# Delta rule of a hybrid decoder: matrix products of three chunks grouped into fewer bursts

## The chip, the cores and the metric

The kernel runs as one program on one core of one Trainium2 chip. The time is the device time of one launch in microseconds, from the first to the last instruction of the program and what lies around them; lower is better. Engines are named as the profile names them: PE is TensorE, DVE is VectorE, ACT is ScalarE, POOL is GpSimd, SP is SyncE.

## What is computed

One step of a one-layer decoder trunk: a projection of 1024 columns in, a mixer with two branches (RWKV-7 time mixing and retention), an output projection, and a mixture of 16 experts. It runs on 528 prompt tokens (16 of them learned) and 8 sample tokens, all in float32. The change lies in the RWKV-7 branch, whose recurrence over tokens is, for each of 8 heads of width 64:

```python
def step(S, inp):
    r_t, w_t, k_t, v_t, kk_t, a_t = inp
    sa = jnp.einsum('bhvk,bhk->bhv', S, -kk_t)
    S = (S * w_t[:, :, None, :]
         + sa[..., None] * (kk_t * a_t)[:, :, None, :]
         + v_t[..., None] * k_t[:, :, None, :])
    y = jnp.einsum('bhvk,bhk->bhv', S, r_t)
    return S, y
```

The state S is returned too. The kernel computes this in chunks of tokens: inside a chunk the tokens' mutual influence is a triangular system, which is solved by an inverse, and only the state goes from chunk to chunk.

## The kernel before

All engines walk through one list of steps, `STEPS`, made by `order()`; each engine does its own part of each step in the order of the list and waits on semaphores for the others. So the order of the list is the order on every engine.

The prompt's 528 tokens make nine chunks: eight of 64 and one of 16 (`CHUNKS`). The 8 heads lie in four pairs, two heads on the 128 partitions. The steps of a chunk c are:

- `wk_e` (ACT): decay factors by exponentials; `wk_p` 0 to 3 (DVE): scaled keys `bk` and the pair of scaled kk and r, `ar`. The last one raises `s_ab`.
- `wk_a` (PE, L1614 to L1632): products of three kinds. The 64x64 matrices between tokens (called A below, L1614), their 32x32 diagonal tiles both ways up (D, L1618 and L1622), and transposes of values and keys (K, L1629 and L1632). DVE then masks D into `tp` (two operations) and A into `ak` (two operations of 128x512); ACT copies K.
- `wk_x` and `wk_t` with b = 2, 4, 8, 16 (X2, T2, X4, ... below): the inversion of the 32x32 tiles by doubling. X (L1643) is 32 products of 32x32 and DVE masks the result; T (L1653 and L1656) is 64 products, at b = 16 only 32, and DVE adds them. Each of these needs the DVE answer to the one before.
- the state chain: `wk_r` (R, L1671 with 128x64 operands and L1676 with 64x64), answered by ACT; `wk_sa` (SA, L1686, upper tiles), ACT; `wk_y` (Y, L1695), DVE; `wk_sb` (SB, L1703, lower tiles), ACT; `wk_s` (S, L1713, L1719 and L1724), answered by DVE with the new state and by ACT with y.

The counts above are the records of the trace: each product of float32 leaves two. The shapes in the trace's rows are those of the weights (rows*columns of the array used) and of the moving data.

The loop runs c from -1 to 7. In an iteration the inversion of chunk c + 1 goes beside the state chain of chunk c. Behind each group of small products ("burst") `take(n, b)` appends n units of other work, "filling": a unit is two products of 128x128 by 128x260 (four records, about 0.88 us), parts of the jobs `j_proj` (L1389), `j_f` (L1425) and `j_bb` (L1402), held in the list `fill`, 146 units in all. `TAKES` says how many units follow each of the nine bursts. When `fill` is empty, `take` gives tiles of branch A, `j_ba` (eight records of L1794). `take` also puts in small steps of `side`: the sample tokens' steps, and the norm behind the recurrence (`j_mean` L1754, `j_var` L1765 and L1761, `ln_r` reciprocals, `j_bc` L1774 and L1779, `ln_b`, `ln_g`). Where c is 5 the loop takes units until a whole job is done; those counted in `owed` are taken off later.

After the loop come the last chunk's R, SA and S, with two takes of two between them, then the rest of `side` by `LAST` with one `j_ba` tile behind each group, then for each of eight tiles the second half of branch A (`j_ba` with 1), which needs all seven parts of the norm (`s_ya`), then the output projection `j_out`, the routing and the experts.

Every DVE operation of the loop is recorded at L2143 or L2146, ACT's at L1893, L2035 and L2056, since helpers make them.

## Time and profile before

| | us |
|---|---|
| median of three runs | 786.96 |
| lowest and highest | 785.82, 788.06 |
| the profiled execution | 785.98 |
| its span, first to last instruction | 784.2 |

| stage, us from the start of the span | what runs |
|---|---|
| 0 to 261 | norm, projections, retention |
| 261 to 515 | the chunk loop |
| 515 to 545 | rest of the norm, branch A |
| 545 to 628 | output projection, routing |
| 628 to 784 | experts, output |

A row of the timeline gives the start, the length (of several instructions: from the first start to the last end), the engine, the line, the operation, out<-in, shapes, the count, and in brackets how long the engine had been idle and who ended that. Lengths of matmuls overlap, so prices are read from the distance of starts.

### The profile page before, as it was taken

The numbers are of one execution on the slowest core, as the hardware profiler recorded it, in microseconds if no ns is written. First come the engines' busy times: TensorE is split into PE (matmuls) and PEld (weight loads), VectorE is DVE, ScalarE is ACT, GpSimd is POOL, SyncE is SP. The second block draws the span as 40 slices with busy tenths as digits, with TensorE's granted clock in tenths as the row PEclk, the third lists the DMA queues.
The fourth block names the chain that finished last, engine by engine and source line by source line (L and its number), as shares of the span: only waits on it lengthen the run. The fifth ranks groups of instructions, "written<-read, shape, count | busy, mean of one in ns | idle before, by whom it ended". The sixth has DMA issues, their size and how long they took to land.

```text
span 784.2 us, 19872 instructions
## 1 busy us (share of the span) xinstructions
PE 751.3 (96%) x8472; PEld 529.5 (68%) x8472; DVE 426.5 (54%) x853; ACT 209.7 (27%) x491; POOL 49.5 (6%) x70
## 2 busy tenths in 40 slices
PE   6999999999999999999999999999999599999995
PEld 5887777787778777777787777778888433333331
DVE  5966667788778574656556565355213432212145
ACT  4222222254525212222222332210031501111144
POOL 0000000000000000010000000000000111221221
PEclk9999999999999999999999999999999789999998
DMA  9562432432211101212422102084934689999965
GB/s 324 191 203 94 148 124 100 178 111 83 79 54 55 55 29 58 69 45 90 129 86 58 55 31 83 13 309 138 413 123 186 237 333 400 393 402 389 370 210 206
DMA packets 38134, 130.43 MB, mean 166 GB/s; under 512 B 6267, under 2 KB 16763, under 8 KB 33184
## 3 DMA queue, kind: packets, MB, share of 16 engines
q1 hardware_dynamic: 32544, 115.07, 39.1%
q0 software_dynamic: 5504, 14.10, 6.1%
q8 instruction: 68, 1.11, 0.6%
q14 instruction: 18, 0.15, 0.1%
HBM read 111.13 MB, written 18.66 MB: 166 GB/s over the span
## 4 chain that ended last, share of the span: by engine, by line
PE 88%; DVE 4%; DMA 4%; issue 2%; ACT 1%; POOL 0%; SPq 0%; POOLq 0%; DVEq 0%; ACTq 0%
PE psum L1444 23%; PE psum L1425 12%; PE psum L1794 10%; PE psum L2740 9%; PE psum L2774 4%; PE psum L1402 4%; DVE arena L2143 3%; PE psum L1377 2%; PE psum L1389 2%; PE psum L1643 2%; PE psum L1656 1%; PE psum L2720 1%; PE psum L1653 1%; PE psum L1614 1%; PE psum L1567 1%
## 5 line engine op out<-in xcount | busy, mean ns | idle before, releaser
L2143 DVE TENSOR_TENSOR arena<-arena 128x268 f32<-128x268 f32 (+13 forms) x322 | 176.5, 548 | 46.3 <-ACT arena L1893 27.6
L1444 PE MATMUL psum<-arena 128*128 128x268 f32 x784 | 188.3, 392 | 0.0
L1444 PEld LDWEIGHTS psum<-arena 128*128 128x128 f32 x784 | 145.3, 189 | 33.3 <-issue 6.7
L1893 ACT ACTIVATE arena<-psum 128x268 f32<-128x268 f32 (+7 forms) x207 | 83.0, 410 | 260.0 <-PE psum L1444 138.6
L1425 PE MATMUL psum<-arena 128*128 128x260 f32 x392 | 101.3, 396 | 0.0
L2143 DVE TENSOR_TENSOR arena<-psum,arena 128x256 f32<-128x256 f32 (+7 forms) x151 | 60.5, 405 | 67.2 <-PE psum L1656 22.5
L1794 PE MATMUL psum<-arena 128*128 128x260 f32 x384 | 88.4, 384 | 1.6 <-DVE arena L2143 1.3
L2740 PE MATMUL psum<-arena 128*32 128x512 f32 (+1 forms) x640 | 87.2, 608 | 0.5 <-DVE arena L2905 0.3
L1794 PEld LDWEIGHTS psum<-arena 128*128 128x128 f32 x384 | 71.1, 189 | 15.3 <-issue 3.2
L2905 DVE TENSOR_TENSOR arena<-psum,arena 128x256 f32<-128x256 f32 (+2 forms) x38 | 24.3, 663 | 103.2 <-ACT arena L2809 90.7
L1425 PEld LDWEIGHTS psum<-arena 128*128 128x128 f32 x392 | 69.6, 189 | 14.4 <-issue 2.8
L1893 ACT ACTIVATE arena<-arena 128x260 f32<-128x260 f32 (+11 forms) x121 | 49.1, 451 | 98.8 <-PE psum L1806 56.2
L2740 PEld LDWEIGHTS psum<-arena 128*32 128x32 f32 (+1 forms) x640 | 25.5, 117 | 58.6 <-issue 58.0
L2146 DVE SCALAR_TENSOR_TENSOR arena<-arena 128x536 f32<-128x536 f32 (+8 forms) x77 | 48.9, 635 | 8.0 <-ACT arena L1893 3.2
L2774 PE MATMUL psum<-arena 128*32 128x512 f32 (+1 forms) x288 | 40.2, 596 | 0.0
L2146 DVE SCALAR_TENSOR_TENSOR arena<-psum,arena 128x260 f32<-128x260 f32 (+2 forms) x23 | 10.1, 441 | 46.9 <-PE psum L1794 40.2
L1402 PE MATMUL psum<-arena 128*128 128x260 f32 x128 | 33.3, 396 | 0.0
L2143 DVE TENSOR_TENSOR arena<-arena,psum 128x260 f32<-128x260 f32 (+4 forms) x35 | 17.6, 514 | 19.7 <-PE psum L1425 16.0
L2146 DVE SCALAR_TENSOR_TENSOR arena<-arena,psum 128x260 f32<-128x260 f32 x32 | 13.7, 427 | 24.2 <-PE psum L1402 12.3
L2809 ACT ACTIVATE arena<-psum 128x256 f32<-128x256 f32 x12 | 4.6, 385 | 79.8 <-PE psum L2740 67.6
L1111 POOL DMA_INDIRECT arena<-u_rows,ids x12 | 12.3, 1022 | 207.7 <-issue 149.8
L2774 PEld LDWEIGHTS psum<-arena 128*32 128x32 f32 (+1 forms) x288 | 10.8, 115 | 21.3 <-issue 21.3
(234 smaller groups left out, 690.9 us busy)
## 6 DMA issues: line engine op xcount, KB each, us to landing
arena<-in_w_gu SPq DMA_DIRECT2D x16, 2048.0 KB, 20.4
arena<-in_w_in SPq DMA_DIRECT2D x45, 512.0 KB, 3.9
arena<-in_w_dn SPq DMA_DIRECT2D x16, 1024.0 KB, 18.2
arena<-in_w_out SPq DMA_DIRECT2D x2, 2048.0 KB, 14.7
arena<-in_x SPq DMA_DIRECT2D x8, 268.0 KB, 5.8
arena<-arena SPq DMA_DIRECT2D x16, 134.0 KB, 4.4
arena<-in_x SPq DMA_DIRECT2D x1, 2144.0 KB, 14.5
arena<-arena SPq DMA_DIRECT2D x4, 520.0 KB, 6.5
```

The costliest lines, as they stand in the source:

```text
L1377: last = mm(ps, wt[:, i, k, :], xg[:, k, cols(hf)], start=(k == 0), stop=(k == KD - 1))
L1389: last = mm(ps, fill_in(0)[side][:, k // 2, k % 2, :], u[:, k, cols2(hf)], start=(k == 0), stop=(k == KD - 1))
L1402: last = mm(ps, bb_tile(m)[:, k, :], ret_o[:, k, cols2(hf)], start=(k == 0), stop=(k == NP - 1))
L1425: last = mm(ps, w[:, k // 2, k % 2, :], x[:, k, :], start=(k == 0 and i in (0, 1, 3)), stop=(k == KD // 2 - 1), skip_group_check=i not in ...
L1444: last = mm(ps, w[:, k, :], x[:, k, :], start=(k == 0 and i in (0, 1, 3)), stop=(k == KD // 2 - 1), skip_group_check=i not in (0, 1, 3))
L1794: last = mm(ps, w[:, k, :], x[:, k, cols2(hf)], start=(k == 0), stop=(k == nk - 1))
L1893: run(nc.scalar.activation(out, in_, fn, **kw), s)
L2143: run(v.tensor_tensor(out, a, b, op), s)
L2146: run(v.scalar_tensor_tensor(out, a, sc_, b, op0, op1), s)
L2740: last = mm(bank(2 + i % 2)[part], ue[:, i % 2, k, part], w_gu[x % NWE][:, k, :], start=(k == 0), stop=(k == KD - 1))
L2774: last = mm(bank(down_bank(e) + q)[part], hht(e)[:, f, part], w_dn[x % NWE][:, f, 512 * q:512 * q + 512], start=(f == 0), stop=(f == 1))
L2905: v.tensor_tensor(out, x, y, op).then_inc(s, 1)
```

## The change

The loop now runs from -2 and an iteration works on three chunks. `bursts(c)` is the table of its five bursts: T16 of chunk c with X4 of c + 1, R of c and K of c + 1; then T4 with SA; Y, D of c + 2 and X8; T8 with X2 of c + 2, SB and A of c + 1; T2 of c + 2 with X16 and S. `wk_a` is split into `wk_k`, `wk_d` and `wk_a`. `TAKES` is three units behind each burst, and two in the iterations ahead of the first state chain. For X the diagonal tiles are copied unmasked into a buffer of their own, `ad` (one more DVE operation a chunk, in `wk_d`); `tp` and `ar` have three buffers in place of two, `e_end` four, the state `st` one. The K transposes go through PSUM banks 2 and 3 instead of 6 and 7. Semaphore counts are now read off the list (`X_N`, `T_N`, `PAB`, `TRI`). The diff, cut to its core:

```diff
-TAKES = (2, 2, 2, 1, 2, 2, 1, 1, 2)
+TAKES = (3, 3, 3, 3, 3)
+TAKES_AHEAD = 2
...
 
-    def solved(c):
-        if c < 0:
-            return [], [], [], [], []
-        w = CHUNKS[c][1]
-        return ([("wk_r", c)], [("wk_sa", c)], [("wk_y", c)] if w > H else [], [("wk_sb", c)] if w > H else [],
-                [("wk_s", c)])
+    def of(c, *steps):
+
+        return [(x[0], c, *x[1:]) for x in steps if 0 <= c < len(CHUNKS)
+                and (x[0] not in ("wk_x", "wk_t") or x[1] < CHUNKS[c][1]) and (x[0] not in ("wk_y", "wk_sb") or CHUNKS[c][1] > H)]
+
+    def bursts(c):
+
+        return [of(c, ("wk_t", 16)) + of(c + 1, ("wk_x", 4)) + of(c, ("wk_r",)) + of(c + 1, ("wk_k",)),
+                of(c + 1, ("wk_t", 4)) + of(c, ("wk_sa",)),
+                of(c, ("wk_y",)) + of(c + 2, ("wk_d",)) + of(c + 1, ("wk_x", 8)),
+                of(c + 1, ("wk_t", 8)) + of(c + 2, ("wk_x", 2)) + of(c, ("wk_sb",)) + of(c + 1, ("wk_a",)),
...
-        w = CHUNKS[c + 1][1]
-        r, sa, y, sb, st = solved(c)
-        lev = [b for b in LEVELS[1:] if b < w]
-        tg = [("tg", i) for i in range(4)] if c < 0 else []
+    for c in range(-2, len(CHUNKS) - 1):
+        tg = [("tg", i) for i in range(4)]
         if c == 0:
             side += samples
-        s += [("wk_a", c + 1)] + take(TAKES[0], 1)
-        s += [("wk_x", c + 1, 2)] + r + take(TAKES[1], 1)
-        s += [("wk_t", c + 1, 2)] + sa
-        s += ([("wk_e", c + 2)] if c + 2 < len(CHUNKS) else []) + take(TAKES[2], 1)
         so = [("so", c + 1 - SMP_FROM, i) for i in range(3)] if 0 <= c + 1 - SMP_FROM < NP else []
-        s += so[0:1]
-        s += [("wk_x", c + 1, 4)] + y + take(TAKES[3]) + tg[0:1]
-        s += [("wk_t", c + 1, 4)] + sb + prep(c + 2, ("wk_p", 0)) + take(TAKES[4], 1)
-        s += [("wk_x", c + 1, 8)] + st + prep(c + 2, ("wk_p", 1)) + tg[1:2] + take(TAKES[5], 1) + so[1:2]
-        if c == 5:
-            while not whole_job():
-                s += take(1)
-            while fill[0][1][0] == "pre" and fill[0][1][2] or fill[0][1][0] != "pre":
-                s += take(1)
-                owed[0] += 1
-            meant[0] = 1
-            assert not side, side
-            s += [("j_mean", n) for n in range(NP)]
-            side[:] = norms(0)
-        if c == len(CHUNKS) - 2:
-            side[0:0] = [("j_mean", 4), ("j_mean", 5)]
-            side += norms(1)
-        s += [("wk_t", c + 1, 8)] + tg[2:3] + take(TAKES[6])
-        if 16 in lev:
-            s += [("wk_x", c + 1, 16)] + prep(c + 2, ("wk_p", 2)) + take(TAKES[7])
-            s += [("wk_t", c + 1, 16)] + prep(c + 2, ("wk_p", 3)) + tg[3:4] + take(TAKES[8], 1) + beside(3) + so[2:3]
-    r, sa, _, _, st = solved(len(CHUNKS) - 1)
+        behind_it = [prep(c + 2, ("wk_p", 2)), prep(c + 2, ("wk_p", 3)) + so[0:1],
+                     ([("wk_e", c + 3)] if c + 3 < len(CHUNKS) else []), prep(c + 3, ("wk_p", 0)),
+                     prep(c + 3, ("wk_p", 1)) + so[1:2]]
+        for i, now_ in enumerate(bursts(c)):
+            if c == -2 and i < 2:
+                continue
+            s += now_ + behind_it[i] + (tg[0:1] if (c, i) == (-2, 4) else tg[1 + i // 2:2 + i // 2] if c == -1 and i % 2 else tg[3:4] if (c, i) == (-1, 4) else [])
+            if i == 4 and c == 5:
+                while not whole_job():
+                    s += take(1)
+                while fill[0][1][0] == "pre" and fill[0][1][2] or fill[0][1][0] != "pre":
+                    s += take(1)
+                    owed[0] += 1
+                meant[0] = 1
+                assert not side, side
+                s += [("j_mean", n) for n in range(NP)]
+                side[:] = norms(0)
+            if i == 4 and c == len(CHUNKS) - 2:
+                side[0:0] = [("j_mean", 4), ("j_mean", 5)]
+                side += norms(1)
+            s += take(TAKES[i] if c >= 0 else TAKES_AHEAD, 1 + (c > 5)) + (beside(3) + so[2:3] if i == 4 else [])
...
-        ar = at(2 * NP * 2 * C, 2, NP, 2, C)
+        ar = [at(NP * 2 * C, NP, 2, C) for _ in range(3)]
         bk = [at(2 * NP * C, NP, 2, C) for _ in range(2)]
         keys = [at(2 * NP * C, NP, 2, C), keys2]
-        tp = [at(2 * NP * H, 2, NP, H), tp2]
+        tp = [at(2 * NP * H, 2, NP, H), tp2, tp3]
         ak = [at(2 * NP * 2 * C, NP, 2, 2, C), ak2]
         vals0 = at(2 * NP * C, NP, 2, C)
-        e_end = at(3 * NP, 3, NP)
-        top[0] += NP * C - 3 * NP
         xl = at(NP * H, NP, H)
-        y1 = at(NP * C, NP, C)
         rr = at(NP * C, NP, C)
-        st = at(2 * NP * C, 2, NP, C)
+        st = at(NP * C, NP, C)
         vals = [vals0, at(2 * NP * C, NP, 2, C)]
+        ad = [at(NP * H, NP, H) for _ in range(2)]
...
+                elif kind == "wk_k":
+                    c = step[1]
+                    t0, w, _, _ = wk(c, 0)
+                    pe.wait_ge(s_ab, c + 1)
                     if c == 0:
                         pe.wait_ge(s_shift, SHIFT_TILES)
+                    else:
+                        pe.wait_ge(s_tri, TRI[("wk_a", c - 1)])
+                    if c >= 2:
+                        pe.wait_ge(s_y1, c - 1)
                     for p in range(NP):
-                        last = nc.tensor.transpose(bank(7, 512, w)[:, p * P:(p + 1) * P], v_f[:, p, t0:t0 + w], ident)
+                        last = nc.tensor.transpose(bank(2, 512, w)[:, p * P:(p + 1) * P], v_f[:, p, t0:t0 + w], ident)
                     last.then_inc(s_px, 1)
                     for p in range(NP):
-                        last = nc.tensor.transpose(bank(6)[:, p * P:(p + 1) * P], bk[q][:, p].rearrange("t a b -> t (a b)"), ident)
+                        last = nc.tensor.transpose(bank(3)[:, p * P:(p + 1) * P], bk[c % 2][:, p].rearrange("t a b -> t (a b)"), ident)
                     last.then_inc(s_px, 1)
                 elif kind == "wk_x":
                     _, c, b = step
-                    l = LEVELS.index(b)
                     if b == 2:
-                        pe.wait_ge(s_tri, 3 * c + 2)
+                        pe.wait_ge(s_tri, TRI[("wk_d", c)])
                     else:
-                        pe.wait_ge(s_tt, LEV0[c] + l - 1)
+                        pe.wait_ge(s_tt, T_N[(c, b // 2)])
+                    if X_N[(c, b)] > 1:
+                        pe.wait_ge(s_xl, X_N[(c, b)] - 1)
                     n = min(CHUNKS[c][1], H)
                     for p, s, d, g, rd in tiles_of(c):
-                        last = mm(psum[g, 2304 + H * p:2304 + H * p + n], ak[c % 2][g, p, s, 0, rd], tp[c % 2][g, 0, p, 0:n],
+                        last = mm(psum[g, 2304 + H * p:2304 + H * p + n], ad[c % 2][g, p, 0:n], tp[c % 3][g, 0, p, 0:n],
                                   start=True, stop=True)
                     last.then_inc(s_pt, 1)
...
-                elif kind == "wk_a":
+                        tt(ar[c % 3][:, :, 1, 0:w], r_f[:, :, x], ep[:, q, :, 1:w + 1], s=s_ab)
+                elif kind == "wk_d":
                     c = step[1]
-                    t0, w, _, _ = wk(c, 0)
-                    dve.wait_ge(s_pab, c + 1)
-                    if c >= 2:
-                        dve.wait_ge(s_ps, 2 * c - 2)
-                    tpc = tp[c % 2]
-
-                    n = min(w, H)
+                    dve.wait_ge(s_pab, PAB[step])
+                    if c:
+                        dve.wait_ge(s_pt, X_N[(c - 1, 8)])
+                    tpc = tp[c % 3]
+
+                    n = min(CHUNKS[c][1], H)
                     tt(tpc[:, :, :, 0:n], bank(4, 256).rearrange("t (a p k) -> t a p k", a=2, p=NP)[:, :, :, 0:n],
                        cc("lev0", 2, H)[:, :, 0:n].unsqueeze(2).broadcast_to([P, 2, NP, n]))
                     tt(tpc[:, :, :, 0:n], tpc[:, :, :, 0:n],
-                       cc("eyeh")[:, 0:n].unsqueeze(1).unsqueeze(1).broadcast_to([P, 2, NP, n]), ALU.add, s=s_tri)
-                    tt(*masked(c, 0), s=s_tri)
+                       cc("eyeh")[:, 0:n].unsqueeze(1).unsqueeze(1).broadcast_to([P, 2, NP, n]), ALU.add)
+                    run(v.tensor_copy(ad[c % 2][:, :, 0:n], psum[:, 2176:2304].rearrange("t (p k) -> t p k", p=NP)[:, :, 0:n]), s_tri)
+                elif kind == "wk_a":
+                    c = step[1]
+                    dve.wait_ge(s_pab, PAB[step])
+                    if c >= 2:
+                        dve.wait_ge(s_ps, 2 * c - 2)
+                    for a in range(2):
+                        tt(*masked(c, a), s=s_tri)
                 elif kind == "wk_x":
...
                     c = step[1]
                     dve.wait_ge(s_rr, c + 1)
                     dve.wait_ge(s_py, c + 1)
-                    tt(y1, psum[:, 1536:1792].rearrange("t (p k) -> t p k", p=NP), rr, ALU.add, s=s_y1)
+                    tt(rr, psum[:, 1536:1792].rearrange("t (p k) -> t p k", p=NP), rr, ALU.add, s=s_y1)
                 elif kind == "wk_s":
                     c = step[1]
-                    q = c % 2
-                    dve.wait_ge(s_ps, 2 * c + 1)
-                    tt(st[:, 1 - q], bank(7, 256).rearrange("t (p k) -> t p k", p=NP), st[:, q], ALU.add)
-                    tt(st[:, 1 - q], st[:, 1 - q], bc(e_end[:, c % 3], C), s=s_st)
+                    dve.wait_ge(s_ps, 2 * c + 2)
```

ACT's part of `wk_a` moves to `wk_k` unchanged but for the bank, and its wait in `wk_e` follows the four buffers of `e_end`.

## Rows read from the trace of the kernel before

**Rows 1.** The page: busy time, 40 slices of the span, a DMA issue.
```profile
PE 751.3 (96%) x8472; PEld 529.5 (68%) x8472; DVE 426.5 (54%) x853; ACT 209.7 (27%) x491; POOL 49.5 (6%) x70
...
PE   6999999999999999999999999999999599999995
...
PEclk9999999999999999999999999999999789999998
...
arena<-in_w_out SPq DMA_DIRECT2D x2, 2048.0 KB, 14.7
```

**Rows 2.** Busy by stage: length, PE, PEld, DVE, ACT, POOL (counts), PEclk, DMA, GB/s.
```profile
342.00:367.90 25.90, 25.88 (x629) 20.60 (x628) 16.41 (x34) 5.84 (x16) 1.69 (x4) 1.00 0.22 64
```

**Rows 3.** Timeline of PE, one period: start, length, engine, line, op, shapes, count.
```profile
355.52 0.48 PE L1656 MATMUL psum<-arena 32*32 32x32 f32 x32
355.81 0.64 PE L1703 MATMUL psum<-arena 32*32 32x64 f32 x16
...
358.34 0.45 PE L1643 MATMUL psum<-arena 32*32 32x32 f32 x32
358.72 0.69 PE L1713 MATMUL psum<-arena 128*64 128x64 f32 x16
...
360.41 2.02 PE L1425 MATMUL psum<-arena 128*128 128x260 f32 x8
362.37 0.45 PE L1653 MATMUL psum<-arena 32*32 32x32 f32 x32
362.64 0.48 PE L1656 MATMUL psum<-arena 32*32 32x32 f32 x32
363.05 1.15 PE L1425 MATMUL psum<-arena 128*128 128x260 f32 x4
```

**Rows 4.** Timeline of PE: its idle waits in the loop, and the longest filling.
```profile
277.38 0.72 PE L1588 MATMUL psum<-arena 128*128 128x268 f32 x2 [0.45 <-DVE arena L2143]
...
285.50 0.45 PE L1656 MATMUL psum<-arena 32*32 32x32 f32 x32 [0.81 <-DVE arena L2143]
...
381.31 0.45 PE L1653 MATMUL psum<-arena 32*32 32x32 f32 x32 [0.17 <-DVE arena L2143]
...
438.07 8.16 PE L1425 MATMUL psum<-arena 128*128 128x260 f32 x36
446.07 2.57 PE L1754 MATMUL psum<-arena 128*128 128x260 f32 x8
...
449.85 0.45 PE L1643 MATMUL psum<-arena 32*32 32x32 f32 x32 [0.53 <-DVE arena L2143]
```

**Rows 5.** Timeline of DVE: operations of the loop, one row for each size.
```profile
274.05 1.24 DVE L2143 TENSOR_TENSOR arena<-arena 128x1040 f32<-128x1040 f32 x1
...
359.98 2.07 DVE L2143 TENSOR_TENSOR arena<-arena 128x256 f32<-128x256 f32 x4
...
366.19 0.29 DVE L2143 TENSOR_TENSOR arena<-psum,arena 128x128 f32<-128x128 f32 x1 [0.70 <-PE psum L1656]
...
369.87 0.43 DVE L2143 TENSOR_TENSOR arena<-psum,arena 128x256 f32<-128x256 f32 x1 [0.71 <-DVE arena L2143]
...
370.79 0.69 DVE L2143 TENSOR_TENSOR arena<-psum,arena 128x512 f32<-128x512 f32 x1
```

**Rows 6.** Timeline of PE behind the loop: last state burst, last broadcast, branch A.
```profile
514.20 0.64 PE L1724 MATMUL psum<-arena 64*64 64x16 f32 x16
...
522.88 1.02 PE L1779 MATMUL psum<-arena 128*64 128x236 f32 x8 [0.39 <-DVE arena L2146]
...
530.61 2.65 PE L1794 MATMUL psum<-arena 128*128 128x260 f32 x11 [1.26 <-DVE arena L2143]
```

**Rows 7.** Timeline of DVE behind the last broadcast: scale, reciprocal, closing operations.
```profile
524.01 0.96 DVE L2491 SCALAR_TENSOR_TENSOR arena<-arena,psum 128x236 f32<-128x236 f32 x2 [0.63 <-PE psum L1779]
...
526.22 0.75 DVE L2481 RECIPROCAL arena<-arena 128x96 f32<-128x96 f32 x1
...
528.35 2.12 DVE L2143 TENSOR_TENSOR arena<-arena 128x472 f32<-128x472 f32 x6
```

109 lines of the change are left out of this document (61 added, 48 removed).

## The prediction, made before the changed kernel was run

> **What bounds the kernel now.** I read the page first. TensorE is busy 96% of the span and at nine tenths in nearly every slice; the chunk loop (about 261 to 515 us) lies in such slices, and the granted clock is full there [rows 1]. Then the busy time by stage: in one period of the loop, from one chunk's first group to the next one's (25.90 us), TensorE is busy 25.88 us, VectorE 16.41 and ScalarE 5.84 [rows 2]. So in the loop only what TensorE itself issues counts, unless another engine answers late. "Busy" hides the loss, since matmuls overlap; it shows in the start-to-start distances of TensorE's timeline, which I read longest.
>
> The price of a burst, from starts alone. Thirty-six large products (128x260) run from 438.07 to 446.07 [rows 4], 0.222 us each, and 0.219 without the delay at their beginning. Eight of them and the way into the next burst take 360.41 to 362.37, 1.96 us, where 8 x 0.219 is 1.75: **0.20 us** is lost around a stretch of large products. Thirty-two 32x32 products take 0.27 us up to more of the same shape (362.37 to 362.64). Thirty-two at L1656 take 0.29 us up to a group of that shape (355.52 to 355.81), but 0.41 up to large ones (362.64 to 363.05): **0.11 us** for leaving the small shape. A join inside a burst costs the same where the shape changes (L1643 to L1713: 0.38 against 0.27), and nothing where it stays 32x32 [rows 3]. So a burst costs 0.31 us beside its own products, a change of shape inside it 0.11.
>
> **What the change does, part by part.**
>
> *Bursts.* I wrote out both step lists. Before, a period has nine bursts (the title's ten isn't what the list holds), and the loop 82: 8 x 9, 7 for the 16-token chunk, 3 at the end. After, it is 3 + 5 + 7 x 5 + 5 + 3 = 51. That is 31 fewer, 31 x 0.31 = 9.6 us. But shape changes inside bursts are added. Per period before: A-D, D-K, X-R, inside R, X-S, inside S, six; after: X-R, inside R, R-K, Y-D, D-X, SB-A, X-S, inside S, eight. Seven periods at two each, one more ahead of them and one fewer at the end are 14 x 0.11 = 1.6 us. Groups joined in one shape (T with X, T with SA or SB) cost nothing. The products are the same in number and size. **Term 1: -8.0 us.** By the same prices a period shrinks from 25.9 us (15 units of four large products, 13.1 us, and 12.8 us of small ones with nine burst costs) to 24.9.
>
> *Waits that get more or less cover.* Each step needs VectorE's or ScalarE's answer to the burst before. Now one or two units of filling (0.88 or 1.75 us) stand between; after, three (2.63 us), two in the first eight bursts. TensorE's idle waits on VectorE in the loop are 0.45, 0.81, 0.17 and 0.53 us [rows 4], about 2.0. The first two come where sums of 1040 elements (1.24 us [rows 5]) are queued ahead of an answer, the third from an operation on the sample group, and the 0.53 from an inversion step with no filling behind it (L1656, then L1643 at 449.85), since units had been taken ahead. All get more filling. What is late next: the first variance product now stands one unit behind the four means of chunk 5, and its squares need VectorE (0.43 [rows 5]) and ScalarE, 0.4 us; and in the first two iterations VectorE's queue holds the long sums, masks and sample work back to back, another 0.4. **Term 2: -2.0 + 0.8 = -1.2 us.**
>
> *VectorE's load.* Added is one copy of 128x128 out of PSUM per chunk, by the 0.29 us of that shape [rows 5]; nine, 2.6 us, cost nothing while VectorE is idle over a third of the period [rows 2]. The heaviest answers: after burst three, y 0.43, the diagonal tiles 0.43 + 0.43 + 0.29 and X's mask 0.29, 1.9 us against 2.63, and y starts when the burst's first group is through. After burst four, T and X 0.7 and two masks of 0.69 [rows 5], 2.1 us, of which the next burst's first groups need the 0.7. After burst five, T and X 0.7 and the state with a preparation step (four operations, 2.07 [rows 5]), 2.8 us, again with the needed ones first. With one state buffer the state's update also waits for all of S, not for its first group only, some 1.2 us later in the burst; behind it on VectorE stand only the preparation and evictions, and R needs it three units on. So each fits. If the cover went, the wait would be the overhang, up to 1 us a period.
>
> *Queues that steps are moved past.* The samples' update (`so`) waits on VectorE for a broadcast that POOL starts. Its first one now stands one burst nearer to the product that feeds it, so VectorE may stand 1 to 2 us once, ahead of evictions that have a burst and three units to catch up: nothing on TensorE, 1 us if that fails. SP's weight loads follow the filling jobs, whose order is kept. The transposes of keys and values (K) wait for masks and for y's read, both bursts old.
>
> *The tail, where the change loses.* Filling is 146 units in both lists. Before, 142 are asked for, and six extra ones at chunk 5 aren't given back, so two tiles of branch A (8 products, 1.75 us each) stand in front of the last state burst. After, 146 are asked for and four extra ones kept, so four tiles stand there, and two fewer remain behind. Before: the state burst's last group starts at 514.20, the last broadcast (L1779) at 522.88, and the second half of branch A at 530.61 after 1.26 us idle behind VectorE's six closing operations of 2.12 [rows 6, 7]. Three tiles stand between the last two; after, three still stand ahead of the broadcast, so that distance stays, and one behind it. VectorE after the broadcast: 1.1 us until it starts (522.88 to 524.01), scale 0.96, reciprocal 0.75 [rows 7], bias 0.96, an eviction 0.43, the closing 2.12 and 0.2 of joins, 6.5 us, where it now is 7.7. TensorE has 2.7 us of work in that time. So the tail behind the state burst gets 1.2 us shorter, with 3.5 us of work moved in front of it. **Term 3: +2.3 us.** Bounds: 0 (if VectorE catches up with the move) and +4 (if the 7.7 us stay and the last mean now waits for the last y).
>
> *Behind it.* The output weights are started after the last state and land 14.7 us after their issue [rows 1]; 14.7 us of tail and eight tiles (14 us) stand before their use. The experts' loads follow branch A. From 530.61 on I shift the trace as it is.
>
> **The sum.** -8.0 - 1.2 + 2.3 = -6.9 us. The profiled execution took 785.98 us (span 784.2), so 779.1. The median of the runs shown is 1.0 higher, 786.96; against that it is 780.0.
>
> **Rivals.**
> A. *Answers come late.* VectorE is one queue, and merged bursts ask it for two or three answers at once. For it: TensorE's idle waits in the loop name VectorE [rows 4]. Against: 16.41 of 25.90 us [rows 2], and cover of 2.63 us. With an overhang of 0.6 us a period, eight periods give back 4.8: 785. **The slower side:** an overhang behind two bursts of each period, 0.7 us each (the 0.81 wait is such a one), is 11 us, 791; it is slower than no change from 9.3 us in all, 1.2 us a period.
> B. *Only changes of shape cost*, 0.11 us each, and the rest of the 0.31 comes back as delay elsewhere. Thirty-one bursts have 62 ends, less 14 added changes 48, 5.3 us for 8.0: 782.7. For it: the 0.11 is seen at exits and joins alike; against, the 0.20 around large products is in the starts of every stretch. The Trainium skill (TensorEngine Tiling, Key Properties) says that a change of the tiling mode drains TensorE while a change of tile in one mode doesn't, which speaks against joining groups of different modes; the trace agrees with the 0.11 at such joins [rows 3].
> C. *The tail costs +4*: 781.7; with half of A mild, 784. Or 0: 777.7.
> D. *The list isn't what I read*, fewer bursts are saved: 1 us per three bursts, say 783. Against: the diff gives the table.
>
> **How the numbers follow.** Forecast (-5.5 to -9 us) 0.62; A mild 0.13, A strong 0.06; B 0.11; C at +4 0.06; D 0.02. The likeliest is 780.0. A mild reaches 785, the good side of terms 2 and 3 776.5; leaving out A strong and the far part of A mild gives 776.5 to 784.5. A measurement of this kernel tells about 0.3%, 2.4 us, from no change. Faster by that: the forecast, B, C, D and half of A mild, 0.87; within 0.07; slower 0.06.
>
> **What would show it.** Five bursts in a period of 24.9 us; 0.11 us at a change of shape and nothing at T-X; idle rows of TensorE in the loop below 1 us in all; 3 to 4 us idle ahead of branch A's second half in place of 1.26. The prediction is wrong if the merged small products start farther apart than now (thirty-two in 0.27 us), if waits on VectorE of 0.5 us recur each period, or if the part behind 530.61 doesn't move along.

## The result, and the profile after

The changed kernel takes 796.48 us, the median of 5 runs (792.47 to 797.54), where the kernel before, run beside it, takes 786.46 (784.73 to 788.06): a ratio of 1.012, 95% interval 1.0089 to 1.0151. Forecast were 780.0 and a range up to 784.5. It is slower by about 1.2%; the sign was wrong, and the miss is 16.5 us.

The profiled execution took 796.48 us. From its page: TensorE's busy share fell from 96 to 94% (compare [rows 1]); q8 is the queue that brings instructions.

```profile
span 794.6 us, 19990 instructions
PE 749.2 (94%) x8472; PEld 533.0 (67%) x8472; DVE 430.1 (54%) x862; ACT 209.1 (26%) x491; POOL 50.1 (6%) x70
PE   7999999999999999899999899998999779999995
PEclk9999999999999999999999999999999879999999
q8 instruction: 68, 1.11, 0.6%
```

Where the 10.4 us of span went, by starts of the same groups in both traces (us):

```
stretch                                          before     after    difference
span's start to the first filling product        255.44    256.91      +1.47
from there to the last group of the last S       258.76    269.20     +10.44   (two tiles of branch A, 3.5, more in it)
from there to branch A's second half              16.41     15.02      -1.39
from there to the end                            253.6     253.5       -0.1
```

The first row is no effect of the change: ahead of the first filling product TensorE's work is the same in both kernels, and in the nine profiles without added instructions that product starts between 255.4 and 256.9 us. The loss is in the loop. First I looked whether the bursts had become dearer. They had not. An undisturbed period of the changed kernel is 25.13 us, TensorE busy throughout, at full clock (start, length, busy time and count of each engine, then clock, DMA share and GB/s); the second stretch lies around the largest pause, the third behind TensorE's idle time ahead of branch A's second half:

```profile
core 0: us, PE busy (x) PEld busy (x) DVE busy (x) ACT busy (x) POOL busy (x), PEclk, DMA share, GB/s
381.36:406.49 25.13, 25.13 (x631) 21.10 (x630) 14.93 (x33) 5.48 (x16) 1.63 (x4) 1.00 0.43 129
331.59:341.18 9.59, 7.24 (x229) 5.80 (x227) 4.01 (x12) 0.22 (x1) 0.00 (x0) 0.82 0.19 60
541.13:545.20 4.07, 4.07 (x11) 3.23 (x12) 0.93 (x3) 0.00 (x0) 0.00 (x0) 0.60 0.95 394
```

The periods before took 25.80 to 26.06. So the bursts are cheaper, as forecast. The loss stands in TensorE's waits. The view of waits, TensorE only, from the loop's start to its end, in the changed kernel (who waited for whom: us in total, times, the longest):

```profile
PE psum L1435 <- DVE arena L2165: 3.1, 3, 1.6
PE psum L1435 <- issue: 2.4, 1, 2.4
PE psum L1598 <- DVE arena L2165: 1.9, 2, 1.7
PE psum L1735 <- issue: 1.5, 1, 1.5
PE psum L1412 <- DVE arena L2488: 0.9, 1, 0.9
PE psum L1661 <- issue: 0.8, 1, 0.8
PE psum L1617 <- issue: 0.6, 2, 0.3
PE psum L1695 <- issue: 0.4, 1, 0.4
```

Before, the same view adds up to some 2.5 us ([rows 4] has the long ones). None of these rows is a small product that waits for its own burst's answer, which is what rival A was about (L1661, L1695, L1617 and L1735 are small products, but before them stands "issue": idle time that nothing in the profile ended). They are of two other kinds.

**Kind 1: the filling waits for VectorE.** L1435 are the large products of the filling. The timeline around the longest such wait:

```profile
373.87 2.02 PE L1435 MATMUL psum<-arena 128*128 128x260 f32 x8
374.05 0.43 DVE L2165 TENSOR_TENSOR arena<-psum,arena 128x256 f32<-128x256 f32 x1 [1.25 <-PE psum L1746]
374.52 2.80 DVE L2165 TENSOR_TENSOR arena<-arena 128x256 f32<-128x256 f32 x5
377.46 1.12 PE L1435 MATMUL psum<-arena 128*128 128x260 f32 x4 [1.57 <-DVE arena L2165]
```

VectorE's five operations are the rest of the state's update (one), a preparation step of the next chunks (two), the sample update `so` (one), and last a sum of two weight tiles (`fs`, 512 elements, 0.69 us), which the filling's products from 377.46 on multiply with. The filling was cover for the bursts in my sum; that it has its own answers to wait for was not in it.

**Kind 2: TensorE stops in the middle of a group, and nothing releases it.** Three of them:

```profile
289.62 0.21 PE L1661 MATMUL psum<-arena 32*32 32x32 f32 x2
290.66 0.45 PE L1661 MATMUL psum<-arena 32*32 32x32 f32 x30 [0.83 <-issue]
332.66 1.15 PE L1435 MATMUL psum<-arena 128*128 128x260 f32 x4
336.15 1.04 PE L1435 MATMUL psum<-arena 128*128 128x260 f32 x4 [2.35 <-issue]
451.73 0.39 PE L1735 MATMUL psum<-arena 128*64 128x64 f32 x5
453.57 0.51 PE L1735 MATMUL psum<-arena 128*64 128x64 f32 x10 [1.46 <-issue]
```

Two of 32 products run, then nothing for a microsecond, then the other 30: missing data is hardly the reason, and e1 below rules it out. The trace has all instruction DMAs: 68 on q8, 16384 B each. TensorE's records (products, weight loads, and instructions that only wait) are 17488, which is 68.3 times 256. I counted them in order of time and set each pause beside the fetch before it (us; "ready until next start" is the time from the fetch's end to that next start):

```
records at   last start   next start   fetch starts   took   ready until next start
the pause
   4033        289.65       290.66        288.37       0.96          1.33
   4289        294.55       295.12        292.76       0.94          1.41
   5057        310.99       311.56        308.98       1.28          1.30
   6081        333.42       336.15        333.85       0.96          1.34
  10177        420.19       420.78        418.40       1.11          1.27
  11713        451.90       453.57        450.76       1.36          1.46
```

The counts differ by multiples of 256 (each is 193 above one), and TensorE goes on 1.27 to 1.46 us after the fetch ends. So instructions come in blocks of 256, and TensorE had used one up before the next was there. The sum of such pauses in the loop is 6.6 us, against 0.6 before, where there is one (0.69 us between starts, at 482.73, count 12993). Over the loop's 44 blocks, the time from the fetch's end to the block's first instruction has a median of 3.75 us before and 2.77 after; 2 blocks before and 9 after have less than 1.6. Two things changed. Blocks became uneven, since the five merged bursts of a period hold 163 to 291 records in 1.2 to 2.8 us (381 to 407 us), three of them in 2.6 us or more, where the nine of before hold 64 to 173 in 0.4 to 2.5: the shortest block lasts 3.75 us before, and 3.38 and 3.65 now. And fetches start later: 3 of 44 before, and 12 now, start more than 2 us after TensorE has entered the block in front; the middle one starts 0.9 us after that before, and 1.2 now, and a few start ahead of it.

Behind the pause of 2.7 us, and behind the 3.36 us of idle time in the tail, the granted clock fell to half (1.2 of 2.4 GHz) for 3.41 us each, an estimated 1.7 us of TensorE's work; the second and the third stretch above show it in their clock, 0.82 and 0.60. The kernel before has no such stretch in either place. (All twelve profiles have a longer one in the experts' part, 17.07 us before and 13.65 after.)

### The profile page after: what moved, and what is told of

Read it like the earlier page. It is cut to its first block, busy times and chain, and to the rows that moved or that the text cites. A ratio compares the mean times of both kernels' runs of the same rounds, so it can differ in the third digit from the quotient of the medians.

```text
span 794.6 us, 19990 instructions
## 1 busy us (share of the span) xinstructions
PE 749.2 (94%) x8472; PEld 533.0 (67%) x8472; DVE 430.1 (54%) x862; ACT 209.1 (26%) x491; POOL 50.1 (6%) x70
## 4 chain that ended last, share of the span: by engine, by line
PE 85%; DVE 5%; DMA 5%; issue 3%; ACT 1%; SPq 0%; POOL 0%; POOLq 0%; DVEq 0%; ACTq 0%
PE psum L1454 21%; PE psum L1435 11%; PE psum L1816 11%; PE psum L2765 9%; PE psum L2799 4%; PE psum L1412 4%; DVE arena L2165 4%; PE psum L1387 2%; PE psum L1399 2%; PE psum L1661 1%; PE psum L1675 1%; PE psum L2745 1%; PE psum L1672 1%; PE psum L1617 1%; PE psum L1577 1%
## 5 line engine op out<-in xcount | busy, mean ns | idle before, releaser
L2165 DVE TENSOR_TENSOR arena<-arena 128x268 f32<-128x268 f32 (+12 forms) x322 | 176.6, 548 | 45.9 <-ACT arena L1915 27.5
L1454 PEld LDWEIGHTS psum<-arena 128*128 128x128 f32 x784 | 145.3, 189 | 33.3 <-issue 6.7
L1435 PE MATMUL psum<-arena 128*128 128x260 f32 x392 | 97.7, 393 | 5.6 <-DVE arena L2165 3.1
L1816 PE MATMUL psum<-arena 128*128 128x260 f32 x384 | 90.1, 390 | 3.7 <-DVE arena L2165 3.4
L1435 PEld LDWEIGHTS psum<-arena 128*128 128x128 f32 x392 | 71.1, 190 | 21.6 <-issue 9.9
L1816 PEld LDWEIGHTS psum<-arena 128*128 128x128 f32 x384 | 72.3, 192 | 18.0 <-issue 5.8
L1915 ACT ACTIVATE arena<-arena 128x536 f32<-128x536 f32 (+11 forms) x121 | 49.0, 451 | 90.7 <-PE psum L1828 58.4
L2765 PEld LDWEIGHTS psum<-arena 128*32 128x32 f32 (+1 forms) x640 | 25.3, 116 | 57.5 <-issue 56.9
L2168 DVE SCALAR_TENSOR_TENSOR arena<-arena 128x536 f32<-128x536 f32 (+9 forms) x77 | 48.9, 635 | 9.9 <-DMA arena<-arena 4.2
L2168 DVE SCALAR_TENSOR_TENSOR arena<-psum,arena 128x260 f32<-128x260 f32 (+2 forms) x23 | 10.2, 442 | 46.4 <-PE psum L1816 40.2
L1412 PE MATMUL psum<-arena 128*128 128x260 f32 x128 | 31.7, 390 | 0.9 <-DVE arena L2488 0.9
L2168 DVE SCALAR_TENSOR_TENSOR arena<-arena,psum 128x260 f32<-128x260 f32 x32 | 13.5, 427 | 27.0 <-PE psum L1816 12.9
L1412 PEld LDWEIGHTS psum<-arena 128*128 128x128 f32 x128 | 23.1, 189 | 5.8 <-DVE arena L2488 1.3
L1340 POOL MEMSET arena<- 64x256 f32 (+1 forms) x18 | 5.5, 312 | 337.9 <-PE psum L1746 205.2
```

Source lines behind the costliest of these rows:

```text
L1412: last = mm(ps, bb_tile(m)[:, k, :], ret_o[:, k, cols2(hf)], start=(k == 0), stop=(k == NP - 1))
L1435: last = mm(ps, w[:, k // 2, k % 2, :], x[:, k, :], start=(k == 0 and i in (0, 1, 3)), stop=(k == KD // 2 - 1), skip_group_check=i not in ...
L1454: last = mm(ps, w[:, k, :], x[:, k, :], start=(k == 0 and i in (0, 1, 3)), stop=(k == KD // 2 - 1), skip_group_check=i not in (0, 1, 3))
L1816: last = mm(ps, w[:, k, :], x[:, k, cols2(hf)], start=(k == 0), stop=(k == nk - 1))
L1915: run(nc.scalar.activation(out, in_, fn, **kw), s)
L2165: run(v.tensor_tensor(out, a, b, op), s)
```

## Experiments

Each kernel is compared with the kernel before, timed in the same job. "Loop" is the time from the first filling product to the last group of the last S (258.76 before, 269.20 after), and "pauses" the sum of pauses at block ends in it (0.6 and 6.6). Each loop and each sum of pauses is read from the one profiled execution of its kernel.

**e1_pad: 64 more instructions ahead of everything**, so that every block ends 64 instructions earlier in the program.

```
-                    pe.wait_ge(s_w[i], 16)
+                    for _ in range(1 if padded else 129):
+                        pe.wait_ge(s_w[i], 16)
+                    padded.append(m)
```

> The changed kernel, with TensorE's wait for its first weights repeated 128 times at the very beginning; nothing else differs, nothing is left out. Theory F (instruction supply): the instruction DMAs on q8 bring 16384 B each, about one per 250 products and weight loads; a merged burst holds 200 to 290 of them in 2.3 to 2.9 us, while 2.3 to 2.8 us pass from the start of such a DMA until TensorE goes on, so TensorE runs out in the middle of groups. 128 more instructions shift every later fetch by about half of its distance: the idle times without a releaser at 289.65 (0.83), 294.55 (0.35), 310.99 (0.30), 333.42 (2.35), 420.19 (0.32) and 451.90 (1.46) go from those products, and others of 0.3 to 2.4 us stand at other places, each ending 2.3 to 2.8 us after the start of a q8 DMA. Rival M (the pause belongs to the group itself, through its shape or its operands): the pauses stay at the same products within 0.2 us. Both: the waits on VectorE (1.57 at 375.51, 0.61 at 416.49, 0.96 at 448.36) stay. Time: F anything from -4 to +4 us around the changed kernel plus 1 to 3 us for the repeated waits; M +1 to +3.

Measured: 797.74 us, ratio 1.0154 (1.0124 to 1.0185). The first product starts at 10.80 us in place of 5.49, since the waits take longer than I had allowed, and the loop takes 265.84, 3.4 us less. None of the old groups is split any more. At count 5057 there is a pause again, but that count now lies 64 instructions earlier in the program: it had split a group of A (L1617), and now splits the group of X (L1665 here) ahead of it in the same burst:

```profile
312.56 0.44 PE L1665 MATMUL psum<-arena 32*32 32x32 f32 x28
314.36 0.22 PE L1665 MATMUL psum<-arena 32*32 32x32 f32 x2 [1.35 <-issue]
```

Its fetch started at 311.89, took 1.21, and was ready 1.25 us before. Pauses add up to 1.8 us. The three waits of the filling on VectorE are the same to 0.01 us (1.955, 0.995 and 1.344 between starts). Rival M, a pause that belongs to its group, is out.

**e2_sums: the last two weight sums go ahead of the burst on VectorE.** In `take`, at its end:

```
+        if fill and fill[0][0] and fill[0][0][0][0] == "fs" and fill[0][0][0][2] >= 2:
+            out.append(fill[0][0].pop(0))
```

> The changed kernel, with the last two of the filling's four weight sums on VectorE put ahead of the burst wherever the list has them right behind one; TensorE's list is the same. Theory V (the filling's own sums are queued behind the burst's answers): the three waits of filling on VectorE, 1.57 us at 375.51, 0.61 at 416.49 and 0.96 at 448.36, go, -3.1 us in all, so about 793.3 where the changed kernel takes 796.5; the burst's own answers come up to 0.7 us later and have 2.6 us of cover. Rival (the answers of the bursts are late themselves): the waits only move to the small products, the time stays within 1 us. The pauses without a releaser stay if they are of instruction supply, since TensorE's instructions are the same.

Measured: 784.98 us, ratio 0.9993 (0.9976 to 1.001). Two lines in the order of VectorE's work give back 11.5 us between the medians (10.0 by the two ratios to the kernel before), where I expected 3.1. The spot of the longest wait, now (L1437 is the filling):

```profile
367.92 2.90 PE L1437 MATMUL psum<-arena 128*128 128x260 f32 x12
368.57 2.07 DVE L2167 TENSOR_TENSOR arena<-arena 128x256 f32<-128x256 f32 x4
370.67 0.43 DVE L2167 TENSOR_TENSOR arena<-arena,psum 128x260 f32<-128x260 f32 x1
```

Twelve products without a wait, since the sum was made ahead of them. All three waits are gone (3.6 us between starts, less the products' own 0.2 each), and with them, against my expectation, most pauses: 2.0 us in place of 6.6, though TensorE's instructions are the same. There is no half clock in the loop, nor in the tail, where the same 3.75 us between starts stand as in the changed kernel (3.74). The spans differ by 11.8 us. Of these, 10.2 lie in the loop (269.20 and 258.96): 3.6 for the waits, 4.6 for pauses and 1.7 for the stretch at half clock make 9.9. Another 1.4 is an earlier start of the loop, ahead of which nothing was changed. The tail's half clock doesn't show as time: the part behind it takes 253.5 us with it and 253.3 without. Why pauses went with waits, two of them show: the fetch for the pause at 420.19 started 0.91 us after the wait on VectorE had ended (417.49 to 418.40), that for 451.90 1.06 after its own (449.70 to 450.76), 3.5 and 4.9 us after TensorE had entered the block, where the middle one of the loop starts 1.2 us after. The largest pause fits too. In the changed kernel a weight load of the filling waits ahead of that place for the sum that VectorE ends at 329.83, 1.4 us after TensorE has entered the block in front at 328.41:

```profile
329.94 0.74 PEld L1435 LDWEIGHTS psum<-arena 128*128 128x128 f32 x4 [0.47 <-issue]
```

There, and in e3 below, whose list is the same up to this point, the fetch starts 5.4 us after that block was entered. In e2, e5 and e6, which have the sums ahead and no such wait, it starts 0.5 to 1.1 us after. So it seems that a wait early in a block holds up the request for the next one, and that the burst behind it uses up what is left. That is an inference from these cases, not shown by a run of its own; e8 tests the other cause of a late fetch.

**e3_tail: two units of filling fewer behind the first two bursts of the last full iteration**, so that two tiles of branch A stand in front of the last state burst, as before the change.

```
-            s += take(TAKES[i] if c >= 0 ...
+            s += take(TAKES[i] - (c == len(CHUNKS) - 2 and i < 2) if c >= 0 ...
```

> The changed kernel, with one unit of filling fewer behind each of the first two bursts of the last full iteration, so that two tiles of branch A stand ahead of the last state burst as before the change, and the list behind it is the same as before the change. If the tail costs what the traces show (the way from the last state group to the second half of branch A is 15.0 us against 16.4 before, two tiles of 1.75 us stand in front, 3.36 us idle in place of 1.26, and TensorE's clock falls to half for 3.4 us behind it): -2 us for the order and -1.7 for the clock, so 792.8 where the changed kernel takes 796.5. Rival (the tail is only shifted, and the experts' loads set what follows): within 1 us of the changed kernel.

Measured: 792.64 us, ratio 1.008 (1.0055 to 1.0105), the total as expected. From the last group of S to branch A's second half it takes 17.18 us, against 15.02 plus the 3.5 us moved in front, 18.5, in the changed kernel and 16.41 before. The clock stays up in the tail. In the loop its pauses are as in the changed kernel (6.7), and so are its waits. But the parts are not as expected: the order gives 1.3 us, not 2, and the part behind it 1.9 (251.6 against 253.5). That this is the half clock isn't shown: e5 below is 1.4 us shorter there than e2, and neither has half clock in the tail.

**e4_split: the same order, each burst cut in two by one of its three units**, ten bursts a period from chunk 0 on.

```
+            cut = (2, 1, 2, 2, 2)[i] if c >= 0 and len(now_) > 1 else 0
+            if cut:
+                s += now_[:cut] + take(1, int(c > 5))
+                now_ = now_[cut:]
...
-            s += take(TAKES[i] if c >= 0 ...
+            s += take(TAKES[i] - (cut > 0) if c >= 0 ...
```

> The changed kernel's order of steps, with each of the five bursts of a period cut in two by one of its three units of filling (ten bursts again, from chunk 0 on). Theory F: a stretch of 256 instructions now always holds large products, so the pauses without a releaser in the middle of small groups go (5.6 us in the changed kernel's loop, under 1 us here). The price of a burst by the prediction, 0.31 us less the 0.11 saved where the cut falls on a change of shape, is paid on about 42 cuts: +10 to +13 us. Sum -5.6 + 11 + (-1 to +1 for VectorE) = +5 us, 801.5 where the changed kernel takes 796.5; clean periods 26.2 to 26.4 us in place of 25.1. Rival M (pauses belong to the groups): they stay, +11 us, 807. Rival B of the prediction (only changes of shape cost): +3 to +5 from the cuts, 794 to 796 under F.

Measured: 794.72 us, ratio 1.0119 (1.0088 to 1.015). The pauses fall to 1.4, nearly as far as F has it (under 1). But the cuts are cheaper than I had them. Without distances over 0.5 us the loop takes 258.5; it has one tile less in it than e2's (1.75) and is still 7.8 us over e2's (252.4 by the same account); for 38 cuts that is **0.21 us a cut**, not 0.31 less a little. (The prediction's own prices give 0.24, since 23 of the 38 cuts take the place of a change of shape.) So the total came out 7 us below the expectation: 3 by the price, the rest by the half clock that isn't there in the loop and by waits of the filling that moved.

**e5_both: e2 and e3 together.**

> The changed kernel with both edits of the runs before: the weight sums ahead of the bursts (785.0, ratio 0.9993) and two units of filling less in the last full iteration. If the tail's order costs what the spans show (from the last state group to the second half of branch A 15.0 us plus the two tiles of 3.5 moved ahead of it, 18.5, against 17.2 with the order of before), it is 1.3 us faster than with the sums alone: 783.7, ratio 0.9975. Rival (the order also decides how what follows runs, since the run with the tail edit alone was 3.8 us faster by its median): 781.2, ratio 0.994.

Measured: **781.92 us, ratio 0.9951 (0.9936 to 0.9966)**, the version that beats both kernels. Its page, and its waits in the loop:

```profile
span 778.4 us, 19994 instructions
PE 744.0 (96%) x8472; PEld 530.9 (68%) x8472; DVE 429.8 (55%) x862; ACT 209.1 (27%) x491; POOL 50.0 (6%) x70
PE psum L1600 <- DVE arena L2167: 1.9, 2, 1.7
PE psum L1414 <- DVE arena L2490: 0.9, 1, 0.9
```

No small product waits, and none stops at a block's end (pauses 0.0; no distance there exceeds the ordinary one by 0.3 us). Periods are 24.91 to 24.98 us, the forecast's 24.9. The loop takes 253.02, and the tail to branch A's second half 17.18. It lies between the two expectations. Of its 3.1 us over e2, 1.3 is the tail's order. The profiled execution also lacks e2's 2.0 us of pauses, and these stand ahead of the edit, where both kernels have the same instructions: whether a fetch comes too late differs from one execution to the next.

**e6_masks: the long operations `tg` (1.24 us) one to two bursts later**, behind the last products of the bonus.

```
-            s += now_ + behind_it[i] + (tg[0:1] if (c, i) == (-2, 4) else tg[1 + i // 2:2 + i // 2] if c == -1 and i % 2 ...
+            s += now_ + behind_it[i] + (tg[i - 1:i] if c == -1 and i else [])
```

> As the run with both edits, and the four VectorE operations on the sums' inputs (tg, 1.24 us each where they are long) stand one to two bursts later, behind the last products of the bonus (j_bon). Theory V: of the 2.04 us and 0.64 us between products at 271.52 and 264.67, where the bonus waits for VectorE, the first falls to 0.5 or less (-1.6), the second stays; 1.5 us faster than the run with both edits, 782.2. Rival (the pause only moves, to the first filling products, which need these operations, or into a fetch of instructions): no gain.

Measured: 782.63 us, ratio 0.9956 (0.9938 to 0.9974), no gain over e5. The distance of 2.04 us fell to 0.76, but one of 1.35 us stands at 289.54, where a burst now waits behind the moved operations, and two pauses are back, 1.4 us. The rival held.

**e7_shift and b2_shift: 64 instructions more at the beginning again**, for e6's kernel and for the kernel before, now as waits on a mark of VectorE that is set at 1.2 us.

```
+                    for _ in range(0 if padded else 128):
+                        pe.wait_ge(s_set, 1)
```

> As the run before it, with TensorE's instruction stream made 64 instructions longer at its beginning (128 waits, two to an instruction, on a mark of VectorE that is set at about 1.2 us, while TensorE still waits for its first weights until 5.5 us). Theory F (pages of 256 instructions): pauses in mid-group stand only where the count of TensorE's records is 193 above a multiple of 256, here 64 instructions earlier in the program than without the shift, so at other groups; their sum may be 0 to 3 us, and the time differs by that difference and by nothing else, -2 to +2 us. Rival (pauses belong to groups): the same pauses at the same groups, the same time within 0.3 us.

> The kernel before the change with the same shift of 64 instructions. Theory F with its reason in the density of small products: before the change a page of 256 instructions lasts 4 to 6 us in the loop and its successor is ready 2 us or more ahead in all but two cases, so the shift changes the time by less than 1 us either way, and the sum of the pauses at page ends stays under 1.5 us (0.7 before). If the shift costs or gains over 2 us here, the pages matter as much before the change, and F is no account of the difference between the two kernels.

Measured: e7 786.15 us, ratio 1.0005 (0.9991 to 1.002), 3.5 over e6, where I expected 2 at most; b2 786.89, ratio 1.0019 (1.0005 to 1.0032). The shift was not free: the first products start at 8.07 us, 2.9 and 2.5 us later, and e7's clock is at half once ahead of the loop. So only the loops can be compared. e7's pauses stand at counts 5057 and 6337, at other groups than e6's, 2.3 us in place of 1.4, and its loop takes 255.73, 1.3 more than e6's; b2's has 0.2 us of pauses, and its loop takes 257.80, 1.0 less than before. So the loops with moved block ends differ by 1 to 3 us from those without in the changed order (e7 and e1), and by 1 in the old one. Which groups are hit follows from the block ends; how much of a difference of 1 us comes from them isn't shown, since pauses of 2.0 us come and go between executions of the same instructions (e2 and e5).

**e8_traffic and b3_traffic: more DMA traffic.** e5's kernel and the kernel before, each with two more DMAs of 512 KB, from DRAM to a buffer in DRAM that nothing reads, behind every weight load of the filling from job pair 2 on.

```
                 sp.dma_start(fill_in(j)[i], x).then_inc(s_w[i if j else 2], 16)
+                for _ in range(2 if j >= 2 else 0):
+                    sp.dma_start(copied[len(junked)], I["w_in"][FILL[j][i]]).then_inc(s_set, 16)
...
```

> The faster changed kernel (weight sums ahead of the bursts, tail as before; 781.9 us, no pause at a page end), with two more DMAs of 512 KB behind each of the filling's weight loads from job pair 2 on: they copy the weights just loaded to a buffer in DRAM that nothing reads, 12 MB in all; the outputs are the same. Five fetches of instructions in the traces so far start within 0.02 us of the last packet of a weight load. Theory L (a fetch waits behind weight traffic): with some 5 us more traffic at each load, fetches of TensorE start up to 5 us later than 0.9 us into their page, and pauses stand at page ends in the loop, 1 to 3 us each, 5 to 15 us in all: 787 to 797. Rival (the coincidence is chance, fetches have their own way): the fetches start as without the traffic, pauses stay under 1 us in all, and the time within 1.5 us of 782 unless a wait for weights appears, which would be named as one.

> The kernel before the change with the same additional copies. Theory L with density: fetches are as late, but a page of the old order lasts 4.5 to 6 us and its successor is ready 2 to 4 us ahead, so fewer of them are missed: pauses of a third to two thirds of those in the changed kernel's order, 788 to 793. If the pauses are as many here as there, the density of the bursts is not what makes late fetches cost.

Measured: e8 795.42 us, ratio 1.0121 (1.0093 to 1.0149), 13.5 over e5; b3 789.59, ratio 1.0052 (1.0032 to 1.0073), 4.2 over the kernel before. Nothing but DMA traffic was added, no wait on VectorE is new in the loop, and the pauses went from 0.0 to 12.0 us in e8 (eight of them) and from 0.6 to 4.4 in b3 (three). Two of e8's and one of b3's (A and S are cut in two):

```profile
338.10 0.71 PE L1626 MATMUL psum<-arena 64*128 64x128 f32 x7
341.42 0.82 PE L1626 MATMUL psum<-arena 64*128 64x128 f32 x9 [2.62 <-issue]
368.63 0.63 PE L1733 MATMUL psum<-arena 32*32 32x64 f32 x16
372.15 1.05 PE L1626 MATMUL psum<-arena 64*128 64x128 f32 x14 [2.90 <-issue]
360.03 0.38 PE L1731 MATMUL psum<-arena 64*64 64x64 f32 x5
362.51 0.56 PE L1731 MATMUL psum<-arena 64*64 64x64 f32 x11 [2.10 <-issue]
```

The fetch for the second started at 369.84, within 0.01 us of the end of a packet of the traffic, of which 3 more started during the fetch, and 5.07 us after TensorE had entered its block; it took 0.93, and 1.38 later TensorE went on. All eight of e8 went on 1.28 to 1.53 us after their fetch. e8's clock fell to half behind three pauses, the two longest and the one of 1.58 us that ends at 291.17. The first two:

```profile
342.00:345.00 3.00, 3.00 (x14) 2.31 (x11) 2.49 (x6) 0.00 (x0) 0.00 (x0) 0.68 0.02 5
372.15:375.50 3.35, 3.35 (x22) 2.79 (x23) 1.98 (x4) 0.53 (x2) 0.00 (x0) 0.74 0.02 5
```

The loops of the two profiled executions, e8's and e5's, differ by 17.7 us; pauses and three stretches at half clock make 17.1 of it. Theory L holds, and so does its half on density: the same traffic costs the old order a third. In the changed kernel itself the largest pause has such a load in front of it: the load issued at 330.71 kept the DMA engines busy from 331.68 to 333.84, and the fetch started at 333.85. The block in front had been entered at 328.41, though, 3.3 us before that traffic began; the wait at 329.94 (see e2) stands between the two, but what held this fetch until 331.68 isn't shown.

## Why the prediction was wrong

- **Term 1, bursts, -8.0 us: the mechanism was right, the size too large.** The periods shrank to 24.9 to 25.1 us from 25.8 to 26.1, as forecast. In e5's loop, everything but distances over 0.5 us is 6.0 us below the kernel before. In place of 0.31 a burst and 0.11 a change of shape, e4's cuts give 0.21 net. The starts show why. Entering small products costs 0.09, the first large product behind them 0.10, leaving small ones 0.12 to 0.15, as priced. But of the joins inside a burst only X to S and D to X cost what was priced (0.12 between starts); the others cost 0.14 to 0.16 us (X to R 0.156, R to K 0.147, SB to A 0.142, Y to D 0.144), and T to X isn't free either (0.044 between starts where products are 0.01 apart). I had taken the price of a join from one place and its zero from one other. Rival B's 5.3 us was closer to the measured 6.0 than the forecast's 8.0, though its reason, that only changes of shape cost, doesn't hold: entering small products costs 0.09 and the first large product behind them 0.10.
- **Term 2, waits, -1.2 us: this step failed.** Distances over 0.5 us cost 15.2 us of the loop in place of 4.0, so +11.2. Of the 15.2, the filling's waits on VectorE are 3.6, pauses at block ends 6.6 (0.6 before), waits in the first iterations 2.2 where I had allowed 0.4, and one behind a copy of the sample state (L2488) 1.0. So term 2 missed by 12.4 us. With the half clock in the loop, 1.7, and the 2 us that term 1 fell short, that is the loop's whole miss, 16.1 us: forecast was -9.2, and measured, without the two tiles, +6.9. Two sentences are at fault. "Each fits" compared VectorE's answers with the cover only for TensorE's small products; the weight sums, which stand in the step list two units ahead of the product that needs them, were never put into the queue, though both lists show them. "Only what TensorE itself issues counts" left out that issuing itself has a supply. The trace of before shows it once: 0.5 us idle in the middle of a group of D (L1622), with no releaser. It isn't in my sum, which lists the waits on VectorE alone.

```profile
482.63 0.28 PE L1622 MATMUL psum<-arena 64*16 64x16 f32 x10
483.42 0.24 PE L1622 MATMUL psum<-arena 64*16 64x16 f32 x5 [0.51 <-issue]
```

- **VectorE's load.** The copy per chunk and the merged answers did fit: in e5, no small product of the chunk steps waits for VectorE. Rival A's mechanism, an overhang of the bursts' answers, didn't occur; that its time for the slower side (791) is the nearest to the result (796) is luck.
- **Queues passed.** `so` (0.7 us) stands in VectorE's queue ahead of the sum that was waited for at 377.46; I had it cost nothing on TensorE.
- **Term 3, tail, +2.3 us: right.** 15.02 plus 3.5 against 16.41 is +2.1; the idle time ahead of branch A's second half was forecast at 3 to 4 us and is 3.36:

```profile
535.75 2.02 PE L1816 MATMUL psum<-arena 128*128 128x260 f32 x8
538.86 2.12 DVE L2165 TENSOR_TENSOR arena<-arena 128x472 f32<-128x472 f32 x6
541.13 5.21 PE L1816 MATMUL psum<-arena 128*128 128x260 f32 x15 [3.36 <-DVE arena L2165]
```

  I had no half clock behind it in the sum. It isn't a certain follower, since e2 has the same idle time and keeps its clock, and no time is seen to hang on it: what follows takes 253.3 us in e2.
- **Behind it.** The part from there on moved along: 253.6 and 253.5 us.
- **The range and the chances.** They held only cases in which a known kind of wait changes its size. The one case that decided, a second queue of answers in the filling and a supply of instructions, had no place in them.

A rule of the Trainium skill bears on this (Runtime: NRT & Kernel Launch, Instruction fetch mechanics). It says that each engine's instruction memory is refilled in blocks of 16 KB, 256 instructions, fetched while the current one runs, and that this is hidden because the sequencer issues more slowly than blocks arrive. The first half is what q8 and the counts show; the second half doesn't hold here: 6.6 us of pauses in the changed kernel, 12.0 in e8. The same section gives TensorE room for 2048 instructions, eight blocks; by the counts, the fetches of all runs here bring the very next block. Of 533 in the loops of the twelve profiles, 261 start 0.85 to 2 us after TensorE entered the block in front, 172 earlier (63 of these ahead of it) and 100 later.

## What to carry to other kernels

Work that is used as cover has inputs of its own: write its answers into the same queue as those of the work it covers, and put an answer ahead of a burst when its product stands within two units behind it. Merging small products into long bursts saves some 0.2 us a burst here, but makes blocks of 256 instructions short, and a late fetch (behind DMA traffic, and perhaps behind a wait early in the block) then shows; look for a group that stops in its middle with no releaser, and count instructions. A pause of that kind moves when anything in front of it is added or removed, and it can come or stay away from one execution to the next, so a difference of 1 to 3 us between two such kernels may be this and nothing else.

## What the runs showed of the hardware

- TensorE's instructions arrive in blocks of 256 (16384 B on q8, 0.9 to 1.6 us each). In the loops of all twelve profiles, no block's first instruction starts less than 1.23 us after its fetch has ended.
- A wait instruction takes room in a block: 128 waits became 64 instructions, and moved every block end by 64.
- Fetches wait for other DMA traffic. e8 and b3 show it by the time. Of the late fetches that ended in a pause, those at 333.85 (changed kernel), 332.80 (e3), 480.94 (before), 339.04, 369.84, 417.87 and 428.50 (e8) and 360.23 and 408.06 (b3) start within 0.01 us of the end of a packet of a load or copy, with at most 25 of its packets left to start during the fetch. For those at 288.37 (changed kernel), 288.32 (e8), 389.54 (e2), 389.12 (e6) and 394.22 (e4) the coincidence says nothing, since a packet ends there every 3 to 12 ns, and 34 to 374 more start during the fetch; the last three stand in copies between buffers, not in a weight load alone.
- 12 MB more of DMA traffic, whose result nothing uses, cost 13.5 us; instruction fetches and the clock account for nearly all of it (17.1 of 17.7 us between the profiled loops).
- In loops and tails, half clock came for 3.41 us at a time, at the end of idle times of TensorE or up to 2 us behind them: 1.35 and 3.36 us (e1), 2.35 and 3.36 (changed kernel), 2.37 (e3), 2.29 (e4's tail), 1.58, 2.62 and 2.90 (e8), 1.88 (b3). It didn't come behind each: not behind the 1.66 of the first iterations in the changed kernel, nor behind 2.10 in b3, nor behind 3.37 in e2's tail.
